# Seven products instead of eight for sixteen of the twenty-two column-tile pairs of a widening projection

## The reference

```python
x = x + merged @ w_o
u = causal_dwconv(rms_norm(x, norm2_g) @ w_up, ffn_conv_w) + ffn_conv_b
u_gate, u_val = jnp.split(u, 2, axis=-1)
return x + (jax.nn.silu(u_gate) * u_val) @ w_down
```

## Time and profile before

| what | value |
|---|---|
| median of 3 runs | 3227.6 us (3226.5 to 3228.28) |
| the profiled execution's own time | 3227.65 us |
| its span, from the first to the last instruction | 3225.9 us |
| TensorE busy | 3185.7 us, 99% of the span |
| VectorE busy | 1962.1 us, 61% |
| ScalarE busy | 721.4 us, 22% |
| mean granted TensorE clock | 0.998 of full speed |

### The profile page before, as it was taken

One profiled execution on the slowest core, in us unless ns is written; L12 is line 12 of the kernel. 1 busy time (PEld: TensorE's weight loads), 2 busy tenths in 40 slices (PEclk: granted clock), 3 DMA queues, 4 the chain that ended last, 5 costly groups with the idle time before them and its releaser, 6 DMA issues.

```text
span 3225.9 us, 44184 instructions
## 1 busy us (share of the span) xinstructions
PE 3185.7 (99%) x16992; PEld 2690.8 (83%) x16992; DVE 1962.1 (61%) x3832; ACT 721.4 (22%) x1624; POOL 123.3 (4%) x221
## 2 busy tenths in 40 slices
PE   8999999999999999999999989999999999999999
PEld 7888888988888889888885644888888888866999
DVE  5678755666783346786863773564446646356576
ACT  2121112121211121210113262211122111145221
POOL 0000000000000000100000010000000000001000
PEclk9999999999999999999999999999999999999999
DMA  6744676556444555564644121553325535232564
GB/s 191 189 111 155 222 226 171 170 159 163 112 146 163 167 152 170 149 189 133 176 143 120 40 53 56 160 189 98 86 85 160 186 111 163 79 112 53 141 176 130
DMA packets 587600, 456.13 MB, mean 141 GB/s; under 512 B 27792, under 2 KB 568880, under 8 KB 587008
## 3 DMA queue, kind: packets, MB, share of 16 engines
q1 hardware_dynamic: 564544, 373.65, 40.2%
q0 software_dynamic: 21376, 77.97, 7.7%
q10 hardware_dynamic: 1472, 1.68, 0.2%
HBM read 452.21 MB, written 1.05 MB: 141 GB/s over the span
## 4 chain that ended last, share of the span: by engine, by line
PE 96%; ACT 1%; DVE 1%; issue 1%; DMA 1%; POOL 0%; ACTq 0%; DVEq 0%; SPq 0%
PE psum L2446 48%; PE psum L2236 38%; PE psum L2243 3%; PE psum L2662 3%; PE psum L2638 1%; PE psum L2597 0%; ACT arena L1527 0%; PE psum L2535 0%; PE psum L2311 0%; PE psum L2473 0%; POOL arena L1203 0%; PE psum L2274 0%; PE psum L2456 0%; PE psum L2262 0%; PE psum L2286 0%
## 5 line engine op out<-in xcount | busy, mean ns | idle before, releaser
L2236 PE MATMUL psum<-hh,ring 128*128 128x256 f32 (+1 forms) x4608 | 1075.3, 393 | 3.3 <-DVE hh L1766 3.0
L2236 PEld LDWEIGHTS psum<-hh,ring 128*128 128x128 f32 x4608 | 872.6, 190 | 180.4 <-issue 69.2
L2446 PE MATMUL psum<-arena 128*128 128x256 f32 (+1 forms) x3520 | 637.1, 338 | 0.3
L2446 PEld LDWEIGHTS psum<-arena 128*128 128x128 f32 x3520 | 562.8, 191 | 56.1 <-issue 1.7
L1547 ACT ACTIVATE arena<-psum 128x256 f32<-128x256 f32 (+1 forms) x544 | 189.0, 347 | 1112.8 <-PE psum L2446 1112.6
L2446 PE MATMUL psum<-arena,ring 128*128 128x256 f32 (+1 forms) x2288 | 415.8, 335 | 2.4 <-ACT arena L1547 2.4
L2446 PEld LDWEIGHTS psum<-arena,ring 128*128 128x128 f32 x2288 | 362.6, 191 | 37.7 <-issue 3.7
L2446 PE MATMUL psum<-hh,arena 128*128 128x256 f32 (+1 forms) x1408 | 295.6, 353 | 0.1
L2446 PE MATMUL psum<-hh,ring 128*128 128x256 f32 (+1 forms) x1408 | 287.1, 356 | 3.3 <-ACT hh L1536 3.3
L2446 PEld LDWEIGHTS psum<-hh,ring 128*128 128x128 f32 x1408 | 241.6, 192 | 36.8 <-issue 5.9
L2446 PEld LDWEIGHTS psum<-hh,arena 128*128 128x128 f32 x1408 | 243.6, 191 | 27.6 <-issue 0.2
(11 more groups left out here) (280 smaller groups left out, 2451.1 us busy)
## 6 DMA issues: line engine op xcount, KB each, us to landing
ring<-in_ffn_w SPq DMA_DIRECT2D x176, 512.0 KB, 5.2
ring<-in_w_in SPq DMA_DIRECT2D x54, 1024.0 KB, 5.3
ring<-in_w_up SPq DMA_DIRECT2D x88, 512.0 KB, 5.3
ring<-in_w_in SPq DMA_DIRECT2D x84, 512.0 KB, 5.3
mod_rows<-in_w_mod_rows POOLq DMA_DIRECT2D x72, 512.0 KB, 3.9
mod_rows<-in_w_mod_late_rows POOLq DMA_DIRECT2D x60, 512.0 KB, 4.9
ring<-in_ffn_w SPq DMA_DIRECT2D x16, 1536.0 KB, 6.7
ring<-in_ffn_w SPq DMA_DIRECT2D x16, 1280.0 KB, 5.9
```

Of the source, the lines that this page charges most:

```text
L2236: ins = mm(o[0:rows_, 0:T], w[:, k, c0:c0 + rows_], src[:, k, 0:T], start=(k == 0), stop=(k == kt - 1))
L2446: ins = mm(o[:, 0:W], lhs[q][:, k, :], src[q][:, k, :], start=(q not in HALF_AFTER and k == 0), stop=(k == n - 1), skip_group_check=q in H ...
```

## The change

In the widening stage of both layers, the pairs i = 2, 3, 4, 5, 7, 8, 9, 10, 12, 13, 14, 15, 17, 18, 19, 20 are made by seven products on token halves, as kind `uph` with `FIRST` in its name. The six others stay as they were. For a pair of the new kind:

- VectorE sums its weights one pair ahead, and once a layer, after the step of pair 0 has begun, makes four sums of the normed input (`hsum1`).
- ScalarE makes four copies as in the other seven-product pairs, and copies product 6 into a buffer `half_val1` too. VectorE's three combinations complete a gate tile and a value tile in SBUF.
- A new step `up_taps` seeds both tiles into `up_buf` from SBUF (ScalarE, scale and bias for each partition), and VectorE adds the two other taps from SBUF. The step stands behind `up_act` of the pair before.

The modulation steps leave the widening stage. The 14 that were there are now made in layer 1's output stage, eight at `sc_out` and six at `att_out`, by the calls of `column_turn` that stood there already without effect; the bias step follows them.

```diff
+SEVEN_UP = [i for i in range(2, FT - 1) if i % 5 != 1]
...
     for i in range(FT + 1):
-        if i < FT:
+        if i + 1 in SEVEN_UP:
+            p.step("wsum", l, FIRST, "uph", i + 1)
+        if i == 0:
+            p.step("hsum1", l)
+        if i in SEVEN_UP:
+            p.half_part(("uph", l, FIRST, i), HALF_ORDER)
+        elif i < FT:
             p.step("up", l, i)
...
         if i >= 1:
             p.step("up_act", l, i - 1)
-            if i < FT - 2:
-                column_turn(p, 2)
+        if i in SEVEN_UP:
+            p.step("up_taps", l, i)
...
+                elif kind == "up_taps":
+                    i = r[0]
+                    name = ("uph", l, FIRST, i)
+                    n = FT * l + i
+                    act.wait_ge(act_ready, n - 1)
+                    evacuated(act, job[(*name, 5)])
+                    for u in range(2):
+                        ch = u * FT + i
+                        src = val_of(name) if u else lead_of(name)
+                        do(nc.scalar.activation(up_buf[:, i % 2, u, :], src, ACT.Identity,
+                                                scale=par("ffn_w", l, ch * FFN_K + FFN_K - 1), bias=par("ffn_b", l, ch)),
+                           up_seeded, 2 * n + u + 1)
...
+                    if kind == "uph" and r[0] == FIRST:
+                        j, m = job[(*name, PROD - 1)], first_names.index(name)
+                        if m >= 2:
+                            act.wait_ge(up_tapped, 2 * m - 2)
+                        produced(act, j)
+                        free(nc.scalar.activation(val_of(name)[:, 0:HALF], bank(j)[:, 0:HALF], ACT.Copy), j)
...
+                elif kind == "up_taps":
+                    i = r[0]
+                    name = ("uph", l, FIRST, i)
+                    for u in range(2):
+                        ch = u * FT + i
+                        src = val_of(name) if u else lead_of(name)
+                        dve.wait_ge(up_seeded, 2 * (FT * l + i) + u + 1)
+                        for d in (1, 2):
+                            o = up_buf[:, i % 2, u, d:S]
+                            ins = stt(o, src[:, 0:S - d], par("ffn_w", l, ch * FFN_K + FFN_K - 1 - d), o, ALU.mult, ALU.add)
...
+                elif kind == "hsum1":
+                    n = 4 * sums_at(l, FIRST)
+                    half = KT // 2
...
+                    do(tt(hf_t1, b12, b11, ALU.subtract), hsum_ready, n + 1)
+                    do(tt(hf_t2, b22, hf_t1, ALU.subtract), hsum_ready, n + 2)
+                    do(tt(hf_t3, hf_t2, b11, ALU.subtract), hsum_ready, n + 3)
+                    do(tt(hf_t4, b21, hf_t2, ALU.subtract), hsum_ready, n + 4)
```

More of the change, by code:

```diff
@@ L866, in build @@
         up_buf = c(2, 2, S)
+        hf_t1, hf_t2, hf_t3, hf_t4 = (c(KT // 2, HALF) for _ in range(4))
+        half_val1 = c(2, S)
         sq_next = arena[:, 81 * S:89 * S].rearrange("p (k t) -> p k t", k=KT)
@@ L1028, in pieces @@
                 src = [(w, P * name[2], P), (w, FFN + P * name[2], P)]
+            elif kind == "uph" and name[2] == FIRST:
+                w = rows(a["w_up"][l])
+                src = [(w, P * name[3], P), (w, FFN + P * name[3], P)]
             elif kind == "mod":
@@ L1110, in lead_of, with val_of @@
             return buf[:, plan.halves[name] % 2, :]
+        def val_of(name):
+            return half_val1[:, plan.halves[name] % 2, :]
         def low_of(name):
+            if name[0] == "uph" and name[2] == FIRST:
+                return val_of(name)[:, HALF:S]
             return wide_low if wide(name) else half_low1 if name[2] == FIRST else half_low
@@ L1119, in build @@
         down_names = [name for name in plan.halves if name[0] == "downh"]
-        up_names = [name for name in plan.halves if name[0] == "uph"]
+        up_names = [name for name in plan.halves if name[0] == "uph" and name[2] != FIRST]
+        first_names = [name for name in plan.halves if name[0] == "uph" and name[2] == FIRST]
         def top_added(name):
@@ L1141, in ffn_at, with sums_at @@
             return 2 * l + w
+        def sums_at(l, w):
+            return l if w == FIRST else DEPTH + ffn_at(l, w)
         mod_t_jobs = [None] + [job[("mod_t", DEPTH - 1, i)] for i in range(len(PIECE_PACKS))]
@@ L1547, in _ @@
                         do(nc.scalar.activation(copy_of(name, q), bank(j)[:, 0:width(name)], ACT.Copy), half_copied, 4 * n + m + 1)
-                    if kind == "uph":
+                    if kind == "uph" and r[0] == FIRST:
[4 more added lines that the diff above has]
+                        free(nc.scalar.activation(val_of(name)[:, 0:HALF], bank(j)[:, 0:HALF], ACT.Copy), j)
+                    elif kind == "uph":
                         evacuated(act, job[(*name, 5)])
@@ L1920, in _ @@
                                 free(ins, j)
+                elif kind == "up_taps":
[8 more added lines that the diff above has]
+                            ins = stt(o, src[:, 0:S - d], par("ffn_w", l, ch * FFN_K + FFN_K - 1 - d), o, ALU.mult, ALU.add)
+                            if d == 1:
+                                do(ins)
+                            else:
+                                do(ins, up_tapped, 2 * first_names.index(name) + u + 1)
                 elif kind == "up_act":
@@ L2025, in _ @@
                     free(tt(lead[:, W:], bank(j3)[:, 0:W], copy_of(name, 2), ALU.add), j3)
-                    if kind == "uph":
+                    if kind == "uph" and r[0] == FIRST:
+                        pass
+                    elif kind == "uph":
                         i = r[1]
@@ L2057, in _ @@
                     do(tt(s[:, 2:4].rearrange("p e m c -> p m e c"), both, twice, ALU.subtract), wsum_ready, e + 1)
+                elif kind == "hsum1":
+                    n = 4 * sums_at(l, FIRST)
+                    half = KT // 2
+                    b11, b12, b21, b22 = h[:, 0:half, 0:HALF], h[:, 0:half, HALF:S], h[:, half:KT, 0:HALF], h[:, half:KT, HALF:S]
+                    do(tt(hf_t1, b12, b11, ALU.subtract), hsum_ready, n + 1)
+                    do(tt(hf_t2, b22, hf_t1, ALU.subtract), hsum_ready, n + 2)
+                    do(tt(hf_t3, hf_t2, b11, ALU.subtract), hsum_ready, n + 3)
+                    do(tt(hf_t4, b21, hf_t2, ALU.subtract), hsum_ready, n + 4)
                 elif kind == "hsum":
-                    n = 4 * ffn_at(l, r[0])
+                    n = 4 * sums_at(l, r[0])
                     half = KT // 2
@@ L2410, in _ @@
                         n = KT // 2
-                        t1, t3, t4 = (h_t1, h_t3, h_t4) if wide(name) else (hh_t1, hh_t3, hh_t4)
+                        t1, t3, t4 = (hf_t1, hf_t3, hf_t4) if w == FIRST else (h_t1, h_t3, h_t4) if wide(name) else (hh_t1, hh_t3, hh_t4)
                         even, odd = h[:, 0:n, :], h[:, n:KT, :]
@@ L2420, in _ @@
                         even, odd = tiles[:, 2 * lo:2 * (lo + n):2, :], tiles[:, 2 * lo + 1:2 * (lo + n):2, :]
-                    src = even[:, :, 0:W], odd[:, :, 0:W], even[:, :, W:2 * W], t3, t1, odd[:, :, W:2 * W], t4
+                    t2 = hf_t2 if kind == "uph" and w == FIRST else even[:, :, W:2 * W]
+                    src = even[:, :, 0:W], odd[:, :, 0:W], t2, t3, t1, odd[:, :, W:2 * W], t4
                     lhs = a11, a12, s[:, 1], s[:, 3], s[:, 0], s[:, 2], a22
@@ L2429, in _ @@
                                 pe.wait_ge(half_asum, sums_of(l, w) + hi)
-                        if kind == "uph" and i == 0 and q in waits:
-                            pe.wait_ge(hsum_ready, 4 * ffn_at(l, w) + waits[q])
+                        if kind == "uph" and i == (SEVEN_UP[0] if w == FIRST else 0) and q in waits:
+                            pe.wait_ge(hsum_ready, 4 * sums_at(l, w) + waits[q])
                         if kind == "downh" and q < 2:
```

12 lines of the change are left out of this document (8 added, 4 removed).

## The result

The changed kernel takes 3240.42 us (median of 5 runs, 3239.73 to 3242.12) against 3228.18 us (5 runs, 3226.5 to 3228.4) for the kernel before: a ratio of 1.004, 95% interval 1.0025 to 1.0055. It is 12.2 us slower; 12.1 were predicted.

The account below looks back on a forecast made before the run. TensorE was taken to bound the kernel; waits of 16.5 us less 10.6 saved make layer 0 5.9 us slower, layer 1 6.2, together 12.1, so 3239.6 us. Its own range was 3235.5 to 3241.5, the forecast's 3231 to 3247.

Parts of the forecast that it names:

- What bounds: Whole kernel: TensorE is busy 99% of the span, so only its microseconds or its waits change the time.
- Saved, 0.66 us a pair: Widening stage: seven products take 6.25 us a pair instead of 6.92, saving 10.6 us a layer, 21.2 in all.
- ScalarE's sum, 1.00 us a pair: Between successive seven-product pairs: ScalarE's chain lasts 2.78 us against 1.79 us of TensorE work, so TensorE waits 1.00.
- the first rival: ScalarE's chain shorter than summed, seeds at 0.416 us: +6.2 us, 3233.8; 13% for a shorter chain, including overlap.
- VectorE late, 1.40 at four pairs and 1.18 at two: Behind activation sums in widening: TensorE waits 1.40 us at pairs 4, 10, 14, 20 and 1.18 at 8, 18.
- The ends: Pair 2 waits 1.36 us (layer 1: 1.61) at the Silu table load; narrowing waits 1.15 behind VectorE's weight sums.
- The sum: Layer 0: waits 16.5 us, saved 10.6, so 5.9 slower; layer 1 6.2 slower; together 12.1 us.
- Moved steps at nothing: Fourteen modulation steps moved to layer 1's output stage cost nothing, TensorE filling its 186 us; uncovered, 19 us.
- The one on the other side: Copy of product 0 ready within 1.79 us, so only pair 2 waits: -18.3 us, 3209.3; chance 11%.
- If ScalarE's instructions had overlapped: ScalarE's back-to-back instructions overlap by about 93 ns: wait 0.46 us instead of 1.00, 2.1 to 2.4 a layer, some 3232.
- the four late pairs: Widening pairs 4, 10, 14 and 20, where VectorE's lateness behind activation sums makes TensorE wait 1.40 us each.
- The clock rival: Waits lower TensorE's granted clock, 3 us a fall; one per group of four pairs +24, 3264; worse-than-summed chance 9%.

Follow-up runs that it names:

- fourteen: Changed kernel with seeds behind the next pair's copy of product 0, early Silu table load, fourteen seven-product pairs in runs of two and three: 3212.74 us, ratio 0.9953.
- late_seeds: Changed kernel with the two tap seeds issued behind, not before, the next seven-product pair's copy of product 0: 3220.41 us, ratio 0.9977.
- third_seed: Changed kernel with one seed of every seven-product pair issued twice, one more ScalarE Identity before the copy: 3253.61 us, ratio 1.0081.
- even_pairs: Changed kernel with only the ten even pairs 2 to 20 made by seven products, each followed by a plain pair: 3221.08 us, ratio 0.9979.
- thin_sums: Changed kernel with the first block's widening weight sums replaced by one addition on a few columns, using stale sums: 3237.68 us, ratio 1.003.
- table_early: Changed kernel with a Silu of one number at the head of each widening stage, loading the table early: 3238.91 us, ratio 1.0037.
- mod_only: Kernel before with only the 14 modulation steps moved from layer 0's widening to layer 1's output stage, all pairs plain: 3227.81 us, ratio 1.0.
- mod_kept: Changed kernel with the 14 modulation steps left in layer 0's widening stage: 3252.39 us, ratio 1.0076.

## Why the prediction was right, by its steps

**What bounds.** TensorE's time or its waits decide: no kernel of the ten experiments speaks against it. In layer 0 of the changed kernel 16.5 us of waits less 10.6 saved are 5.9, and 6.24 were measured.

**Saved, 0.66 us a pair.** Shown by `fourteen`: 6.91 against 6.26, and 8.98 of the 9.2 us of fourteen pairs came out as time.

**ScalarE's sum, 1.00 us a pair.** 1.01 at the pair read above. That it is this chain and its order is shown three ways: shorter by two seeds the wait of these pairs is gone (`late_seeds`), longer by one seed it grows by that seed (`third_seed`), and with the neighbours gone it is gone (`even_pairs`, where the list has two waits left in layer 0, at the two ends of the stage). The seed, for which the earlier trace rows had no instruction at its place, is 0.600 us; the lower bound of 0.416 and with it the first rival fall. The Trainium skill ("ScalarE: Activation LUTs", What ACT_TABLE_LOAD costs) is right on the operands' price in this kernel (two of some 93 ns by it, 0.600 less 0.416 here), and its overlap of 93 ns is not to be seen where each instruction waits for the one before: starts are the duration and 0.035 us apart (503.24, 503.88, 504.51). Where ScalarE waits for nothing in between it is there: before, two squares of 0.62 us at 1305.29 are followed by the next at 1306.35.

**VectorE late, 1.40 at four pairs and 1.18 at two.** 1.42 at pair 10. Pair 8 begins its product 2 at 495.95 where 494.82 would do, 1.13 and 0.07: 1.20. Without the weight sums both shrink to the ScalarE value (a bracket of 0.78 in `thin_sums`). VectorE is not the bound with a plain pair every fifth, and is with none.

**The ends.** Pair 2: product 2 starts at 453.12, where products 0 and 1 from 450.12 would make room at 451.91; 1.21 and 0.07 is 1.28 (1.36 predicted). `table_early` gives 1.14 and 1.24 of it back, a little less than the 1.3 expected. The narrowing's first wait is 597.10 - 596.00 = 1.10, and 0.07: 1.17 (1.15 predicted), at the end of the chain of weight sums, two taps, Silu and copy that was named.

**The sum.** +6.2 and +6.5 for +5.9 and +6.2. The 0.3 a layer is small and has one likely home: 16 pairs of 6.26 instead of 6.25 are 0.2 of it. I have not measured it apart. The stage lasts 157.1 us (436.23 to 593.32), as given. That the medians differ by 12.2 where 12.1 was said is in part luck: the two layers hold 12.8, and the rest of the kernel moves by more than the difference.

**Moved steps at nothing.** Shown by `mod_only`; 186 us of TensorE in 186 with them, and no wait for a row load there. Loads of `w_up` in layer 0 land in 5.1 us instead of 5.4; with the steps moved alone it is 5.2, and in layer 1 before, which had no row loads beside them, 5.1.

**Rivals.** The one on the other side, that the copy is ready within 1.79 us, would have needed the copy early; its start lies 2.31 us behind the pair's end (502.80 in ScalarE's timeline, 500.49) where 1.29 was the latest (1.79 less 0.22 and the copy's 0.28). Where the order puts it at 1.18 (`fourteen`, 503.93 against 502.75) the waits are gone, as that rival had it. If ScalarE's instructions had overlapped, the prediction has 2.1 to 2.4 us a layer, without the terms; with the four late pairs at 1.64, as TensorE then comes to them 0.54 earlier, I estimate some 2.7, which would have been no change as well. The clock rival: about 1 us without matmuls in every 7.3 left the granted clock at 1.00 over both stages. The Trainium skill ("TensorE: Matmul & The Clock Gate", A second HAM failure mode) tells of a clock that oscillates with short idles; of the changed kernel's stages this is not true. Where waits reached 3.6 and 5.3 us (`mod_kept`) it fell, and cost 1.5 us each time: half of what that rival had set down for a fall.

## What to carry to other kernels

Before giving the bottleneck engine shorter work, list what stands in the in-order queue of the engine that must answer it, in program order, between its last instruction and the answer. A saving per item smaller than that list's excess over the cover (here 0.66 against 1.00) is a loss, and then the cure is the order, not the saving: the same instructions behind the answer instead of ahead of it were worth 20 us here. After that, add the second engine's work over a whole turn; it decides how many items in a row can be changed (three of four, not nineteen).

## What the runs showed that I had not expected

`fourteen` was forecast at 3209.6 us and took 3212.74. Its two layers are 17.8 us faster, as forecast within 0.4; the rest is lost in code that no edit touched. One place is visible, at the start of the second block's attention. The same 16 matmuls, in `fourteen` and, in the second fence, before:

```profile
1892.48 3.56 PE L2719 MATMUL psum<-arena 128*64 128x256 f32 x16 [0.32 <-ACT arena L1745]
```

```profile
1909.86 1.95 PE L2638 MATMUL psum<-arena 128*64 128x256 f32 x16 [0.31 <-ACT arena L1689]
```

The granted clock of those 4 us was 0.57 (mostly at the 1.2 GHz level), and 1.00 before; ahead of it TensorE was busy 5.29 of 7 us, and before it was the same 5.29 of 7 (1902.40 to 1909.40):

```profile
1885.00:1892.00 7.00, 5.29 (x34) 3.13 (x32) 6.28 (x15) 5.28 (x12) 0.00 (x0) 1.00 0.67 214
1892.00:1896.00 4.00, 3.68 (x20) 1.98 (x18) 2.09 (x6) 2.56 (x7) 0.00 (x0) 0.57 0.00 0
```

That is 1.6 us. Why the clock fell there in one kernel and not in the other, behind the same work, stays open, and so does the other microsecond: the rest of the span is 1916.2 to 1919.0 us over twelve kernels whose second blocks are the same, and I found no rule in which of them had more. A gain of 3 us in one stage could not be told by the whole time of such a kernel; it can by the distance of two marks around the stage.
